# Attention stages: VectorE's scale of the last piece moved ahead of the mask and maximum of the next

## What is computed

```python
# NSA, per query head (g: sigmoid gates)
s = einsum('...rqnl', qi, kg) * scale        # selected keys, masked
p = softmax(where(mask, s, NEG)); o_s = p @ vg
s_w = einsum(qb, kb) * scale                 # window keys, masked
p_w = softmax(where(mask_w, s_w, NEG)); o_w = p_w @ vb
o = g[0] * o_c + g[1] * o_s + g[2] * o_w
# MLA, per head
o = causal_block_attention(q, k, v, MLA_QK ** -0.5)
```

## Time and profile before

| | |
|---|---|
| median of 3 runs | 6980.02 us (6978.0 to 6980.3) |
| profiled execution, its own time | 6981.36 us |
| its span | 6979.8 us |
| busy over the span | TensorE 5304.5 us (76%), VectorE 3317.5 us (48%), ScalarE 1167.3 us (17%), GpSimd 311.0 us (4%) |
| MLA, 5670 to 5790 us (first loop) | TensorE 100.52, VectorE 71.62, ScalarE 50.41 us of 120, granted clock 0.91 |
| MLA, 5809 to 5926 us (second loop) | TensorE 98.65, VectorE 71.61, ScalarE 50.30 us of 117, granted clock 0.93 |

### The profile page before, as it was taken

One profiled execution on the slowest core, in us unless ns is written; L12 is line 12 of the kernel. 1 busy time (PEld: TensorE's weight loads), 2 busy tenths in 40 slices (PEclk: granted clock), 3 DMA queues, 4 the chain that ended last, 5 costly groups with the idle time before them and its releaser, 6 DMA issues. The chain is left out here.

```text
span 6979.8 us, 89810 instructions
## 1 busy us (share of the span) xinstructions
PE 5304.5 (76%) x35968; PEld 4046.1 (58%) x35968; DVE 3317.5 (48%) x4305; ACT 1167.3 (17%) x1835; POOL 311.0 (4%) x192
## 2 busy tenths in 40 slices
PE   6787882499639896766668699676477977879988
PEld 4677881398518685234347588433444544658876
DVE  8436666544454574746564522324344445532233
ACT  2102222222222000300002200110122333111100
POOL 0000001211100000200000000002000000000000
PEclk8898996699869997578878899875566678989999
DMA  1221003411131452241413222243111011422233
GB/s 67 85 78 49 27 24 145 173 52 58 52 136 62 145 187 89 83 170 37 160 60 110 79 96 96 79 127 106 28 27 23 4 34 36 145 85 72 72 119 125
DMA packets 269305, 593.92 MB, mean 85 GB/s; under 512 B 33628, under 2 KB 132827, under 8 KB 268300
## 3 DMA queue, kind: packets, MB, share of 16 engines
q1 hardware_dynamic: 197704, 412.19, 18.0%
q10 hardware_dynamic: 55360, 120.08, 4.5%
q0 software_dynamic: 15968, 57.78, 2.3%
HBM read 397.78 MB, written 192.19 MB: 85 GB/s over the span
## 5 line engine op out<-in xcount | busy, mean ns | idle before, releaser
L385 PE MATMUL gu_ps<-kept_h_hi,gu_w_hi 128*128 128x512 f32 x704 | 274.8, 390 | 39.6 <-DVE gu_w_lo L118 39.6
L385 PE MATMUL gu_ps<-kept_h_lo,gu_w_hi 128*128 128x512 f32 x704 | 274.6, 390 | 0.0
L385 PE MATMUL gu_ps<-kept_h_hi,gu_w_lo 128*128 128x512 f32 x704 | 274.5, 390 | 0.0
L385 PE MATMUL win_ps<-kept_hn_hi,win_w_hi 128*128 128x512 f32 x576 | 225.4, 391 | 39.7 <-DVE win_w_lo L118 39.7
L3275 PE MATMUL be_ps<-be_hi,be_w_hi 128*128 128x512 f32 x512 | 202.8, 396 | 59.2 <-DVE be_lo L118 58.7
L385 PE MATMUL win_ps<-kept_hn_lo,win_w_hi 128*128 128x512 f32 x576 | 225.1, 391 | 0.0
L385 PE MATMUL win_ps<-kept_hn_hi,win_w_lo 128*128 128x512 f32 x576 | 225.0, 391 | 0.0
L3275 PE MATMUL be_ps<-be_lo,be_w_hi 128*128 128x512 f32 x512 | 200.6, 392 | 0.0
L3275 PE MATMUL be_ps<-be_hi,be_w_lo 128*128 128x512 f32 x512 | 200.4, 391 | 0.0
L2220 PE MATMUL lc_ps<-idft,lc_zz 128*128 128x256 f32 x512 | 121.8, 404 | 90.1 <-DVE lc_zz L2100 63.1
L420 DVE COPY win_o<-win_ps 128x1024 f32<-128x1024 f32 x36 | 44.1, 1225 | 286.9 <-PE win_ps L385 286.9
(11 more groups left out here) (650 smaller groups left out, 13125.8 us busy)
## 6 DMA issues: line engine op xcount, KB each, us to landing
rk_in<-s_decayed SPq DMA_DIRECT2D x8, 3072.0 KB, 16.0
oproj_mod_w<-in_ada_w POOLq DMA_DIRECT2D x12, 2048.0 KB, 9.2
gu_w<-in_w_gu SPq DMA_DIRECT2D x44, 512.0 KB, 3.5
win_w<-in_w_in SPq DMA_DIRECT2D x36, 512.0 KB, 3.5
s_z<-win_o ACTq DMA_DIRECT2D x36, 512.0 KB, 2.6
s_decayed<-rkp_ring SPq DMA_DIRECT2D x32, 512.0 KB, 2.7
dn_kv<-s_qkv SPq DMA_DIRECT2D x16, 768.0 KB, 6.0
oproj_w<-in_odd_w SPq DMA_DIRECT2D x24, 512.0 KB, 5.1
```

Source lines behind the costliest of these rows:

```text
L385: mm = pe.matmul(ps[:, u, h, :], a, b, start=(k == 0 and n == 0), stop=(k == kt - 1 and n == len(pairs) - 1))
```

## The change

In step n VectorE first does reciprocal and scale of piece n-1, which wait for the exponential of n-1, and then mask, maximum and `nb` of piece n.

```diff
@@ -2820,6 +2820,14 @@
                 if nbuild:
                     dve.wait_ge(built, nbuild * (i + 1))
                 for n in range(NPC + 1):
+                    if n >= 1:
+                        m = n - 1
+                        gate, w, s = flat[m][6], flat[m][7], m % 3
+                        dve.wait_ge(expd, NPC * i + m + 1)
+                        dve.reciprocal(rs[:, s:s + 1], sm[:, s:s + 1]).then_inc(inv, 1)
+                        dve.wait_ge(inv, NPC * i + m + 1)
+                        dve.tensor_scalar(pr[:, s, 0:w], pr[:, s, 0:w], rs[:, s:s + 1], gate if gate is not None else 1.0,
+                                          ALU.mult, ALU.mult).then_inc(scaled, 1)
                     if n < NPC:
                         _, _, _, _, mask, _, _, w = flat[n]
                         s = n % 3
@@ -2830,14 +2838,6 @@
                         dve.reduce_max(mx[:, s:s + 1], sb[:, s, 0:w], AX.X).then_inc(maxed, 1)
                         dve.wait_ge(maxed, NPC * i + n + 1)
                         dve.tensor_scalar(nb[:, s:s + 1], mx[:, s:s + 1], -scale, None, ALU.mult).then_inc(nb_ready, 1)
-                    if n >= 1:
-                        m = n - 1
-                        gate, w, s = flat[m][6], flat[m][7], m % 3
-                        dve.wait_ge(expd, NPC * i + m + 1)
-                        dve.reciprocal(rs[:, s:s + 1], sm[:, s:s + 1]).then_inc(inv, 1)
-                        dve.wait_ge(inv, NPC * i + m + 1)
-                        dve.tensor_scalar(pr[:, s, 0:w], pr[:, s, 0:w], rs[:, s:s + 1], gate if gate is not None else 1.0,
-                                          ALU.mult, ALU.mult).then_inc(scaled, 1)
```

## The result

The changed kernel took 7020.32 us (median of 4 runs, 7016.44 to 7030.77) against 6979.01 us (6977.67 to 6980.3) for the kernel before, run beside it. The ratio is 1.0063, with a 95% interval of 1.0048 to 1.0079: slower by 41 us. The forecast was 7005 with a range of 6992 to 7030, so the sign and the range hold, and the loss is 16 us larger than the sum.

The account below looks back on a forecast made before the run. TensorE was taken as the bound, with VectorE mostly waiting for its scores. Steady MLA heads 12.6, steady NSA heads 3.6 and loop starts 8.8 make 25.0 us over 6980.02, so about 7005, range 6992 to 7030.

Parts of the forecast that it names:

- the sum: Both attention stages: late masks add 12.6 + 3.6 + 8.8 = 25.0 us; band 6994 to 7018, chance 0.62.
- the serial chain: Rival: TensorE not the bound, all 192 pieces lose their cover, 188 us more, 7168; chance 0.04.
- The gain of 0 for the earlier scale: Transposes on TensorE: the copy releases them after the scale, so gain 0, bounds 0 and 46.6 us.
- The tail, exponential + scale + 0.43: VectorE, both stages: the next mask can start exponential + scale + 0.43 us after `nb`; earlier scores make it late.
- A steady MLA head loses 2.06: MLA masks late by 1.05 at 640 columns, 0.1 at 768, 0.91 at 896; six steady heads, 12.6 us.
- NSA's steady head loses 0.6: NSA: only small pieces make the mask late, 0.6 us a head; six steady heads, 3.6 us.
- The clock term, taken as 0: TensorE's granted clock in both stages: new stalls might shift it; 0 in the total, -8 to +24 us for the range.
- a granted clock that moves by more than 0.02: Sign that the forecast is wrong: TensorE's granted clock changes by more than 0.02 in either attention stage.
- The four loop starts, 8.8: First heads, two loops per stage: masks late, 1.7 us each in NSA, 2.7 in MLA, 8.8 us together.
- The rival *clock: New stalls add one clock fall of 1.5 us in each of 16 heads, 24 us more: 7029; chance 0.20.
- faster: Rival: the scale releases the transposes, so 46.6 us come back against 25.0: 6958; chance 0.05.
- absorbed: Rival: TensorE's slack in later pieces takes up the late masks, less than 14 us left: 6987; chance 0.09.

Follow-up runs that it names:

- the covered order alone: Kernel before, with the new VectorE order only at pieces whose tail the wait for TensorE covers (also called covered_only): 6973.85 us, ratio 0.9995.
- the three pieces named: Kernel before, with the new VectorE order only at MLA's 640, 768 and 896 columns: 6985.7 us, ratio 1.0011.
- the pairs with filler: Four unused matmuls in MLA's wait ahead of the transposes of 896 columns, in the changed kernel (7017.85 us) and the kernel before (6986.22 us).
- MLA alone: New VectorE order in the MLA stage, NSA as in the kernel before: 7004.39 us against 6978.08, ratio 1.0035.
- nsa_only: New VectorE order in the NSA stage, MLA as in the kernel before (also called NSA alone): 6993.11 us, ratio 1.0021.
- the copy first: ScalarE's copy of piece n-2 moved ahead of the exponential of n: 6828.5 us in VectorE's old order, 6874.16 new, 6805.66 new only at covered pieces.
- the filler in NSA: Four unused matmuls in each of two NSA waits ahead of small transposes: kernel before 6979.77 us, changed kernel 7023.27 us.

## Why the prediction held, and where it was off

- *What bounds the kernel.* TensorE does, as read from the earlier trace rows: all 128 new NSA waits of VectorE together cost TensorE 1.6 us of idle time. The rule of the Trainium skill, in "Perfetto Trace Analysis", section "Identifying the Most-Contended Engine", to judge TensorE's headroom by its weight-load share, by which the serial chain would have gained, did not hold here: after the change VectorE still waited 145.9 us for TensorE in NSA.
- *The gain of 0 for the earlier scale.* Right: the covered order alone made no difference. The sign that TensorE's waits for the copy grow by some 17 us came true, but nearly all of it in MLA (16.0, and 1.4 in NSA). Of the sign that weight-load waits for the scale vanish, half came true: 1.9 us left in MLA (23.1 before), but 29.1 in NSA (23.5 before). As before they are no loss, since the matmuls beside them waited 0.8. Why they grew in NSA was not followed up.
- *The tail, exponential + scale + 0.43.* Right: the masks came late by 1.04 at 640 columns (forecast 1.05), and by 0.58 at the 256-column window piece of an NSA head (0.57; 7.50 us into the head before, 8.08 after).
- *A steady MLA head loses 2.06.* Right in size (1.92 and 2.0 at equal clock), wrong in one place. The sentence that at 1024 columns VectorE's wait covers the tail failed; taken alone, the three pieces named make only 1.1 us, and the 0.9 at 896 stays lost through the mask of 1024 behind the scale of 896.
- *NSA's steady head loses 0.6.* The mask of 512 is late by 0.86 (16.31 us into the head before, 17.17 after), 0.3 more than forecast. The wide pieces add no wait, as forecast; but the head is 1.7 us longer (64.91 to 66.63).
- *The clock term, taken as 0.* This is the term of the sum that failed. It came to about 16 us: 8.6 in MLA by the pairs with filler, and some 8 in NSA, what is left of 15 when the forecast's waits (3.6 + 2 x 1.7 = 7.0) are taken off, up to 13 if one goes by TensorE's idle time, which grew by 1.6 alone. In MLA all four heads between the first and the last of a loop have a fall where two of four had one (three of four in the profile of MLA alone), and the last heads of the loops went from 1.00 to 0.92. Outside the loop starts MLA's grant falls to 0.50 eight times instead of two; six more at 1.62 us would be 9.7, an estimate beside the 8.6. In NSA no fall is new in the head shown; the clock that rises again inside it rises later, after 37.5 us instead of 30.8. The argument against it, a high grant over MLA, spoke of how seldom falls were, not of how near to one each head stood; and a stage at 0.65 has its own clock to lose. The sign "a granted clock that moves by more than 0.02" came up in MLA (0.90 to 0.86).
- *The four loop starts, 8.8.* The first head of each MLA loop grew by 3.3 and 5.2 us against the 2.7 forecast, but at another clock than before (0.68 to 0.75, and 0.76 to 0.68). The runs with filler, old order and new, have this head at the same clock:

```profile
5673.40:5696.46 23.06, 21.81 (x79) 11.87 (x79) 17.03 (x38) 8.72 (x23) 0.00 (x0) 0.76 0.00 1
...
5680.54:5707.65 27.11, 23.40 (x83) 12.29 (x82) 18.23 (x40) 10.15 (x26) 0.00 (x0) 0.76 0.00 1
```

That is 4.05 more. Of these, 1.47 are the mark at which the head is taken to end: the next mask of 128 started 0.86 after `nb` of 1024 (5889.36 to 5890.22) and now starts 2.33 after it (5926.81 to 5929.14), behind the scale of 1024. What is left, 2.6, is about the forecast's 2.7. In NSA the first head of `nsa_only` takes 62.62 us and that of `covered_only`, where the loop start has the old order, 60.99, both at 0.65: 1.6 more, forecast 1.7. The term held.
- *The size of the whole.* 25 of waits, confirmed at 17.1 of 18.0 for MLA; NSA's 7.0 rest on the mask times and the one pair of first heads. The split of NSA's 15 is the least sure part: the interval of that run alone is 8 to 21 us.

The rival *clock* gave 7029, with a fall in each of 16 heads at 1.5 us. By the forecast's own bands, 7020 lies in that rival's (7018 to 7040, chance 0.20) and not in that of the sum (6994 to 7018, chance 0.62): the range held because it took in part of the rival's band. In MLA the rival's mechanism is what was seen, a fall in nearly each head at 1.6 us; in NSA stretches at 0.50 grew longer instead. *Serial*, *faster* and *absorbed* are out.

## What to carry to other kernels

In a software pipeline written by hand, an engine with long waits for another one is not free everywhere: find the pieces where its wait is shorter than the chain that you move into it, and follow each delay through everything that stands behind it in order (here the copy behind the exponential) to the engine that sets the pace, one piece further than where it first shows. Test an order on every queue of the chain, not only on the one in question: the early scale was worth nothing, or a loss of 46 us, or a gain of 23 us, depending on the order on ScalarE and on where it was used. Where TensorE's granted clock is below 1, don't put a change in its waits down at their length.

## What the runs showed of the hardware

Gaps in TensorE's work can cost far more than their length. With the copy first TensorE was idle 31.8 us less in the two stages (12.6 in NSA, 19.2 in MLA), and the stages took 146.8 us less, since the granted clock of NSA's steady heads went from about 0.7 to 1.00 and the same head from 64.91 to 45.05 us. The sum of the gaps does not decide it: the filler in NSA filled 20 us of idle time (64.4 to 44.2) and gained nothing.

The level doesn't follow from one wait or from how busy TensorE is at the time. Before the change TensorE worked 28.00 of 28.00 us at 0.50. And in MLA the same wait ahead of the same seven transposes was followed by the lower clock in one head and not in another; both from the timeline of the kernel before:

```profile
5726.38 1.58 PE L2795 MATMUL mla_ppt<-mla_ident,mla_p 128*128 128x128 f32 x7 [2.45 <-ACT mla_pt L2857]
...
5891.63 0.96 PE L2795 MATMUL mla_ppt<-mla_ident,mla_p 128*128 128x128 f32 x7 [2.46 <-ACT mla_pt L2857]
```

Four matmuls that nobody reads, put into that wait, removed the fall in each of the four heads between the first and the last of a loop, with either order. What decides between the two levels in NSA was not found. The runs of NSA's filler with the old order also scattered more than others: they lay within 55 us, those of the kernel before, in all experiments, within 21 (6967.35 to 6988.58), and those of NSA alone within 21.
